# Attention outputs written feature-major, and two modulation vectors moved to TensorE

## What is computed

```python
mod = silu(c) @ w_ada + b_ada                  # six vectors of 1024 per sequence: shift, scale, gate, twice
h = rms_norm(x, g_attn) * (1 + scale_a) + shift_a
q_a, k_a, v_a, c_q, c_kv, k_r = split(h @ w_in)
q_a, k_a = rope(rms_norm(q_a)), rope(rms_norm(k_a))     # 8 query heads, 2 key heads of 64
o_a = softmax(q_a k_a^T / 8) v_a                        # group A
q_b = rms_norm(c_q) @ w_uq        # 8 heads: 64 plain columns, 32 that are then rotated
kv  = rms_norm(c_kv) @ w_ukv      # 8 heads: 64 key columns, 64 value columns
k_b = [k_nope, rope(k_r)]         # the rotated 32 are shared by the heads
o_b = softmax(q_b k_b^T / sqrt(96)) v_b                 # group B
o = concat(rms_norm(o_a, g_out_a), rms_norm(o_b, g_out_b)) @ w_o
x = x + gate_a * o
h = rms_norm(x, g_ffn) * (1 + scale_f) + shift_f
u = conv3(h @ w_up) + conv_b      # 5632 columns
x = x + gate_f * ((silu(u_gate) * u_val) @ w_down)
```

## Time and profile before

| | |
|---|---|
| time, median of 3 runs | 1193.37 us (1190.86 to 1193.6) |
| the profiled execution's own time | 1194.76 us |
| span in its profile, first to last instruction | 1193.0 us |
| busy: TensorE, its weight loads, VectorE, ScalarE, GpSimd | 98%, 84%, 61%, 45%, 48% |
| mean granted TensorE clock | 0.986 of full speed |

### The profile page before, as it was taken

How to read it: one execution, slowest core, us unless ns; L and a number is a source line. 1 busy time by engine, 2 the same in 40 slices (tenths; PEclk the granted TensorE clock), 3 DMA queues, 4 the chain that set the end, 5 groups by cost and what they waited for, 6 DMA issues and landing times.

```text
span 1193.0 us, 18770 instructions
## 1 busy us (share of the span) xinstructions
PE 1165.8 (98%) x6288; PEld 997.4 (84%) x6288; DVE 728.9 (61%) x1481; ACT 534.5 (45%) x866; POOL 568.4 (48%) x768
## 2 busy tenths in 40 slices
PE   9999999999999999999999999999999999999997
PEld 6897887998888888888789979889888888888886
DVE  5878986767766677757666438746775134412345
ACT  5347675254431344234354677635543234422432
POOL 2487500655655445644665540054555544454462
PEclk9999997999999999999999999999999999999998
DMA  9743333423445444544433202222343322332322
GB/s 350 307 168 116 92 103 107 141 72 132 174 139 207 133 166 176 194 141 176 141 110 119 75 1 89 89 89 71 124 141 106 106 86 90 106 106 74 102 89 71
DMA packets 43979, 151.55 MB, mean 127 GB/s; under 512 B 5122, under 2 KB 7810, under 8 KB 43908
## 3 DMA queue, kind: packets, MB, share of 16 engines
q1 hardware_dynamic: 43908, 150.64, 36.6%
HBM read 148.52 MB, written 2.10 MB: 126 GB/s over the span
## 4 chain that ended last, share of the span: by engine, by line
PE 46%; issue 24%; POOL 15%; POOLq 6%; DVE 6%; DVEq 2%; ACT 1%; ACTq 0%
POOL w_lo L535 14%; PE ps L614 14%; PE ps L620 14%; PE ps L615 14%; POOLq L536 5%; DVE ada_prod L1387 2%; DVEq L1389 1%; DVE nmx L1758 1%; PE ps L749 1%; PE ps L950 1%; PE ps L738 1%; PE ps L718 0%; DVE ada_prod L1608 0%; DVE o_sb L1771 0%; PE ps L726 0%
## 5 line engine op out<-in xcount | busy, mean ns | idle before, releaser
L535 POOL TENSOR_TENSOR w_lo<-w_raw,w_hi 128x256 fp32r<-128x256 f32 x712 | 532.1, 779 | 599.3 <-ACT w_hi L1117 575.7
L614 PE MATMUL ps<-h_hi,w_hi 128*128 128x512 f32 (+1 forms) x960 | 349.7, 364 | 4.2 <-DVEq L1561 2.2
L615 PE MATMUL ps<-h_lo,w_hi 128*128 128x512 f32 (+1 forms) x960 | 347.3, 362 | 0.0
L620 PE MATMUL ps<-h_hi,w_lo 128*128 128x512 f32 (+1 forms) x960 | 347.2, 362 | 0.0
L1117 ACT CAST w_hi<-w_raw 128x1024 fp32r<-128x1024 f32 x178 | 183.2, 1047 | 183.8 <-PE ps L614 183.6
L614 PEld LDWEIGHTS ps<-h_hi,w_hi 128*128 128x128 f32 x960 | 181.7, 189 | 36.8 <-DVEq L1561 3.8
L1809 DVE SCALAR_TENSOR_TENSOR u_sb<-ps,par,u_sb 128x510 f32<-128x510 f32 x176 | 131.7, 748 | 123.2 <-ACT u_sb L1345 110.2
L620 PEld LDWEIGHTS ps<-h_hi,w_lo 128*128 128x128 f32 x960 | 181.7, 189 | 27.5
L615 PEld LDWEIGHTS ps<-h_lo,w_hi 128*128 128x128 f32 x960 | 181.8, 189 | 27.2
L614 PE MATMUL ps<-a_hi,w_hi 128*128 128x512 f32 (+1 forms) x400 | 146.6, 366 | 3.3 <-DVEq L1595 2.4
L620 PE MATMUL ps<-a_hi,w_lo 128*128 128x512 f32 (+1 forms) x400 | 145.6, 364 | 0.0
(11 more groups left out here) (160 smaller groups left out, 1372.6 us busy)
## 6 DMA issues: line engine op xcount, KB each, us to landing
w_raw<-w_slots SPq DMA_DIRECT2D x178, 512.0 KB, 3.5
ada_raw<-ada_slots SPq DMA_DIRECT2D x88, 512.0 KB, 3.8
shift<-shift_slots SPq DMA_DIRECT2D x8, 512.0 KB, 13.2
x_tok<-x_rows SPq DMA_DIRECT2D x4, 512.0 KB, 9.6
x<-x_t SPq DMA_DIRECT2D x4, 512.0 KB, 13.7
y_t<-x SPq DMA_DIRECT2D x3, 512.0 KB, 2.9
y_t<-x SPq DMA_DIRECT2D x1, 256.0 KB, 3.0
y_t<-x SPq DMA_DIRECT2D x2, 128.0 KB, 2.7
```

Source lines behind the costliest of these rows:

```text
L535: nc.gpsimd.tensor_tensor(w_lo[:, j, c], w_raw[:, j, c], w_hi[:, j, c].bitcast(F32), ALU.subtract)
L614: hh = mm(out, stat[0], mov[0], start=first, stop=False)
L615: hl = mm(out, stat[0], mov[1], start=False, stop=False)
L620: return mm(out, stat[1], mov[0], start=False, stop=last)
```

## The change

**Outputs feature-major.** In `outputs` the roles are swapped: the values (64 columns) are the stationary operand and the transposed probabilities the moving one, so a pair gives 128 feature rows (64 for each head of the pair, in column groups 0-63 and 64-127 of the array) by 256 tokens. The column of ones is gone: the exponentials accumulate their row sums (`accum_out`), and VectorE divides the probabilities, 1024 per partition in one instruction, before they are transposed (`scale_rows`). The transposes wait for that; TensorE's step is now `scores(i)`, `fill(i+1)`, `prob_transposes(i-2)`, `outputs(i-3)`.

**Group B's queries and keys** are made feature-major by the projection itself (w_uq is the stationary operand, with the rotated columns twice, swapped in the second copy), so that `fill` is gone for group B, and its scores are two accumulating products with 64 rows each instead of one with 96. GpSimd's rotation and VectorE's copies change accordingly; VectorE also takes the query, key and (one) value copies from ScalarE.

**The group norm** needs no transposes: GpSimd adds squares (`add_squares`), TensorE sums them over features with products of one column (`group_sums`), ScalarE takes the root per token, VectorE the reciprocal, TensorE spreads it over the partitions (`group_spread`), and VectorE scales (`output_scaled`). Output tiles 0 to 3 now have a bank each; their first halves (group A's rows) are computed first, the second halves follow one after the other.

**Modulation.** Layer 0's gate A and shift F (16 slots) leave VectorE: in steps 1 to 8 of layer 0's attention TensorE multiplies two slots per step in four column groups of 32 (`stream_products`), ScalarE copies the partial sums, and TensorE adds the four groups with a selecting product (`stream_select`). VectorE's remaining slots move from attention to layer 0's feed-forward part.

```diff
-ORDER = [(0, SCALE_A), (0, GATE_A), (0, SHIFT_F), (0, SCALE_F), (0, GATE_F),
+ORDER = [(0, SCALE_A), (0, SCALE_F), (0, GATE_A), (0, SHIFT_F), (0, GATE_F),
+STREAMED = (2, 3)
-    plan = [(("in", 1), 6, 2), (("in", 2), S_UQ, 2)]
-    plan += [(("unit", i), S_WO - 1, 1) for i in range(NP + 1)]
-    plan += [(("wo", m), S_WO + m, 1) for m in range(1, TAIL)]
-    ups = [[1] * 8, [1, 2, 1, 2, 1, 2, 1, 1], [2, 2, 1, 1, 1, 0]]
+    plan = [(("in", 1), 6, 2), (("in", 2), S_UQ, 1), (("in", 3), S_UQ, 1)]
+    plan += [(("stream", i), S_WO - 1, 1) for i in range(N_PE)]
+    plan += [(("wo", m), S_WO + m, 1) for m in range(TAIL)]
+    ups = [[1, 2, 1, 2, 1, 2, 1, 2], [2, 2, 1, 2, 1, 2, 1, 2], [2, 2, 2, 2, 1, 0]]
-    plan += [((1, "unit", i), SLOTS + S_WO - 1, 1) for i in (7, 8, 9, 10, 11, 13, 14, 15)]
...
     for m in range(TAIL):
-        take(("wo", m), 4 + m % 2)
+        take(("wo", m), m)
     for i in range(N_UPD - TAIL):
         take(("wo_half", i), HALF_BANKS[i % 3])       # (4, 5, 2), unchanged
...
-            width = 4 * QK_B                          # 384 columns, 48 products
+            for n in range(HEADS):                    # 512 columns, 48 products
+                        last = product(ps[:, bank(key), :], [r[:, j, at:at + P] for r in (w_hi, w_lo)],
+                                       [r[:, k, :] for r in (ct_hi, ct_lo)], k == 0, k == 1, ...)
...
+                            p, at = heads[0] // 2, s * SEQ + q * P
+                            parts = [(qn[:, p, at:at + P], kn[:, p, c]), (qr[:, p, at:at + P], kr_t[:, c])]
+                        for n, (st, mv) in enumerate(parts):
+                            for u in range(2):
+                                r = slice(64 * u, 64 * u + 64)
+                                last = mm(ps[:, S_BANK[j % 2] + u, q * SEQ:(q + 1) * SEQ], st[r], mv[r], start=n == 0,
+                                          stop=n == len(parts) - 1)
...
                     pe.wait_ge(pt_ready, NP * L + j)
+                    pe.wait_ge(rows_scaled, NP * L + j + 1)
...
-                    for u in range(2):
-                        for q in range(2):
-                            for k in range(2):
-                                last = mm(ps[:, O_BANK, c:c + VW], prob_t[:, j % 2, u, k, q * P:q * P + P], v,
-                                          start=(k == 0), stop=(k == 1))
+                    for k in range(2):
+                        for u in range(2):
+                            last = mm(ps[64 * u:64 * u + 64, O_BANK, 0:SEQ], v, prob_t[:, j % 2, u, k, :],
+                                      start=(k == 0), stop=(k == 1))
...
+                def stream_products(h):
+                    pe.wait_ge(part_taken, h)
+                    for r in range(2):
+                        k = K_PE + 2 * h + r
+                        pe.wait_ge(ada_landed[k % 4], 16 * (k // 4 + 1))
+                        for g in range(4):
+                            last = mm(ps[32 * g:32 * g + 32, QT_BANK, 0:SEQ], c_pad[:, 4 * r + g, :],
+                                      ada_raw[:, k % 4, g * SEQ:(g + 1) * SEQ], start=r == 0, stop=r == 1)
+                        last.then_inc(ada_streamed, 1)
...
+                def scale_rows(j):
+                    dve.wait_ge(exp_ready, 4 * (NP * L + j + 1))
+                    V.reciprocal(rinv[:, j, :], rsum[:, j, :])
+                    V.drain()
+                    V.tensor_tensor(prob[:, j % 2], prob[:, j % 2],
+                                    rinv[:, j, :].rearrange("p (c o) -> p c o", o=1).broadcast_to([P, 4, SEQ]),
+                                    ALU.mult).then_inc(rows_scaled, 1)
```

More of the change, by code:

```diff
@@ new lines, in _ @@
+                pe.wait_ge(ct_ready, 3 * L + 2)
+                for n in range(HEADS):
+                    j = slot(L, S_UQ + n // 4)
+                    key = ("uq", n)
+                    wait_free(pe, L, key)
+                    for k in range(2):
+                        at = (n % 4 * 2 + k) * P
+                        last = product(ps[:, bank(key), :], [r[:, j, at:at + P] for r in (w_hi, w_lo)],
+                                       [r[:, k, :] for r in (ct_hi, ct_lo)], k == 0, k == 1,
+                                       {0: 2, 4: 1}.get(n, 0) * int(k == 0))
+                    last.then_inc(full[bank(key)], 1)
+                    if n == 3:
@@ new lines, in stream_select @@
+                def stream_select(h):
+                    pe.wait_ge(part_taken, h + 1)
+                    for f in range(2):
+                        at = h % 4 * 2 * NSEQ + f * NSEQ
+                        last = mm(stream_sums(h // 4)[:, at:at + NSEQ], part_sb(h)[:, f * P:f * P + P], sel, start=True,
+                                  stop=True)
+                    last.then_inc(stream_full, 1)
+                expand_values(0)
+                fill(0)
+                expand_values(1)
@@ new lines, in _ @@
+                    if i == NP + 1:
+                        out_part(L, 0, (0, 1))
+                        group_sums(1)
+                    if 0 <= i - 2 < NP:
+                        prob_transposes(i - 2)
+                    if L == 0 and 0 <= i - 1 < 4 * len(STREAMED):
+                        stream_products(i - 1)
+                    if 0 <= i - 3:
+                        outputs(i - 3) if i < NP + 2 else None
+                    if i == NA + 3:
+                        group_sums(0)
@@ L985, in _ @@
+                    if i == NA + 4:
+                        group_spread(0)
+                out_part(L, 0, (2, 3))
+                group_spread(1)
+                outputs(NP - 1)
+                out_part(L, 1, range(KD // 2))
+                group_sums(2)
+                out_part(L, 2, range(KD // 2))
+                group_spread(2)
+                out_part(L, 3, range(KD // 2))
+                for m in range(TAIL):
+                    out_part(L, m, range(KD // 2, KD), int(m > 0))
                 norm_tail(2 * L + 1, lambda m, s, release: half_out(L, m, s, release))
@@ L1250, in _ @@
                 wait_full(act, L, "krt")
-                nc.scalar.copy(kb_t[NOPE:QK_B, 0, :], ps[NOPE:QK_B, bank("krt"), :])
+                nc.scalar.copy(kr_t[:], ps[:, bank("krt"), :])
                 nc.scalar.drain()
```

706 lines of the change are left out of this document (405 added, 301 removed).

## The result

The changed kernel takes 1223.73 us (median of 4 runs, 1222.51 to 1224.76) against 1193.48 us (1190.86 to 1195.81) for the kernel before: a ratio of 1.0254, with a 95% interval of 1.0229 to 1.0278. The profiled execution spans 1220.7 us (before 1193.0), so 27.7 us are to be found in it.

What follows compares the result with a forecast made beforehand. TensorE, busy 98% of the span, was taken as the bound. Savings of 11.3 us (layer 1) and 5.6 (layer 0), 16.9 in sum, less 4.5 for the clock, gave about 1181 us; forecast case 1174 to 1187, full range 1166 to 1193.

Steps and rivals of the forecast that it cites:

- The slots in layer 0's feed-forward part: Modulation slots moved into layer 0's feed-forward part cost nothing, as VectorE was busy 59.7 of 86 us there.
- The sign that I gave: Idle TensorE in layer 0's up tiles would show the forecast wrong.
- a price if the cover were gone: Layer 0's feed-forward part: each moved slot would cost up to 2.4 us (twice 1.22) if VectorE's time were not covered.
- Group A's sums and spread: TensorE's norm products for group A, inside group B's steps of the attention: 1.8 us.
- group B's step: TensorE's attention step in group B: scores 2.1, transposes 0.88, outputs 1.0, in sum 4.0 us in place of 4.78.
- Behind the last scores: Last scores to first half tile: 34.2 us in each layer, against 42.9 (layer 0) and 36.9 (layer 1) before.
- The clock term: Low-clock stretches after TensorE waits over 1 us at five places (both attentions' starts and ends, the bank): 4.5 us taken.
- The bank wait in layer 0's output projection: TensorE waits 5.2 us for bank 4 before the fourth half tile, until VectorE's first half-tile update at 22.0 us.
- Query projection: Its 48 products widen from 384 to 512 columns and cost 2.7 us per layer.
- Missing overlap: Rival: column groups do not overlap, outputs stay at 1.73 us, 20 us in sum, 1201 us; chance 0.06.
- mode switches: Rival: entering and leaving tiled form costs 0.2 us, 56 times, 11 us, giving 1189; chance 0.18 with longer waits.
- The slow rival: TensorE's clock stays at 1.2 GHz through group A's attention steps: 1217 us for all, 1205 for two thirds; chance 0.1.

Runs made afterwards that it cites:

- run 1: The kernel before with only the eight modulation slots moved from layer 1's attention into layer 0's feed-forward up tiles (one more vector halved): 1211.48 us, ratio 1.0163.
- run 3: The changed kernel with the same sum of layer 0 feed-forward slots spread over up and down tiles: 1203.31 us, ratio 1.0087.
- run 7: The changed kernel with run 3's and run 5's edits, group A's spread one step later, end-of-attention reorders, no slot behind last up tiles: 1184.19 us, ratio 0.9923.
- run 5: The changed kernel with the rounding of the next weight slot ahead of the square in ScalarE's list behind the attention: 1222.86 us, ratio 1.0252.
- run 8: Run 7 with layer 0's four modulation slots moved from behind the first output tiles into attention steps and VectorE's spread wait: 1179.17 us, ratio 0.9887.

## Why the prediction was wrong

**The slots in layer 0's feed-forward part (costed at nothing): the step that failed.** "One or two slots more per eight tiles leave it under TensorE's time" was read from a mean: 59.73 of 86 us busy in the earlier trace rows. But that window holds up and down tiles, and the change put its slots into the up tiles. There a tile of TensorE gives VectorE 10.9 us, and it needs 6.2 without a slot (9.04 less 2.8, its waits for ScalarE among them) and 2.8 for each. By that eight tiles hold 13.4 slots (8 x 4.7 / 2.8); two copies of silu(c) and the end of a vector take some 4 us more, which leaves about 12. The change put in 12 and 13, after 8 and 11. The step should have been made per tile, and for the last one with what stands behind it: the bank of the first down tile. The sign that I gave, idle TensorE in layer 0's up tiles, looked at the wrong place too: the up tiles kept their 87.0 us, and the down tiles paid. I had even given a price if the cover were gone, up to 2.4 a slot, 19 for the eight; I gave that case no chance, and the waits and the clock behind them made it more. Measured: +23.4 in the changed kernel, +21.2 from this edit alone (run 1), all but 4.2 of it taken back with as many slots in other places (run 3).

**Group A's sums and spread (1.8 us, no wait).** I priced the products and not what a product in TensorE's ordered list waits for. The chain of exponentials, table load and reciprocal cost a wait of 3.7 us a layer and, with what follows the wait at the lower clock, 6.3 and 5.4 us: nearly all of the 6.8 and 6.0 us by which the stretches of the scores are over the forecast. In run 7, with the spread one step later, it is 72.9 and 62.1 us; the forecast was 72.4 and 61.5. The prices of outputs and steps were near, that of group B's step through two errors that cancel.

**Behind the last scores (34.2 us forecast, 38.9 in both layers).** The waits came as foreseen, 1.15, 2.19 and 0.22 us against 1, 2 and 0.5. What was missing is what follows them: the window 180 to 200 us has a granted clock of 0.83, and a group of transposes and an output together take 3.8 us (192.93 to 196.71) instead of 2.0. With the waits shortened by run 7's orders it is 34.8. The clock term, 4.5 us for five places, was too small: waits of 3.7 us in the scores cost 6.3 and 5.4 us, and some 6 us of waits at each of the two stalls in the feed-forward part cost 8.7 and 8.4, about half as much again as the wait. The wait of 2.00 us in run 3, with no low clock behind it, cost 1.8 (46.0 us of down tiles instead of 44.2). That the addition is the clock is read from the rows; no run tested it by itself.

**The bank wait in layer 0's output projection (+5.2).** The size was near (+6.4) by luck, for the wait itself did not come. VectorE's time up to its first half-tile update was right (21.6 us, 213.61 to 235.18, for 22.0), but GpSimd, which splits a weight slot in 4.94 us beside VectorE's slots, held TensorE twice (2.13 and 2.12 us) before it wanted the bank. Once GpSimd started earlier (run 5), a bank wait showed, 2.22 us. Run 8 shows that both come from the modulation slots: without them the stretch is back at 43.6 us.

**Query projection, streams, slots before the latent parts.** +2.3 for 2.7 in layer 1. In layer 0 it is +2.3 too, counted from the first squares (57.71 to 103.56, before 59.78 to 103.35); that only +0.2 is left comes from the start, which varies by such 2 us between runs of the same lists.

**The rivals.** Missing overlap did not show (outputs at 1.01 us), nor did the 8 us that I gave mode switches beyond the forecast. That a switch costs something is not excluded: transposes between tiled products take 1.02 us where they took 0.88. The slow rival named the clock over group A's steps; the clock fell elsewhere, after waits (1.00 from 105 to 160 us). What the stretches took beyond their forecasts comes to 23.4 + 12.8 (scores) + 9.3 (behind them) = 45.5 us; with the small rows of the table, -0.8 in sum, and less the 4.5 that I had set against the clock, that is the 40 us between the forecast span of 1180.6 and 1220.7.

## What to carry to other kernels

Work that is moved onto a half-busy engine must be set against that engine's time in the very tile that it joins, with the fixed work and its own waits, and above all in the last tile before another engine needs something of it; a mean over a window that holds two kinds of tile hides a full engine. A small product in TensorE's list costs what its input waits for: try the consumer of a cross-engine chain one step later before doing anything to the chain, and look at what this delays in turn. In these traces a TensorE wait of 4 to 6 us cost about one and a half times its length. And when a change loses, take its parts apart: with its lists reordered (run 7) the new attention took 96.9 us in layer 1 from the first scores to the first half tile, where 96 were forecast and 109.7 stood before, and the version of run 8 beats both kernels.

## What the hardware showed that I had not expected

GpSimd's subtraction of a weight slot (four of 256 columns) takes 2.82 us alone, 3.3 beside VectorE's updates and square sums (run 8), and 4.94 beside VectorE's products of two fp32 operands of 1024 columns, which themselves take 1.56 instead of 1.23 us (changed kernel, 216 to 233 us). The kernel before had such slots too (4.97 us at 221.56). The Trainium skill (SBUF — State Buffer, Who interferes with whom) says that the two engines share a pair of ports under an exclusive lock; the trace agrees in that both engines' instructions grow; which of them waits it doesn't show.
